# A twelve-stage network on one core: fill matmuls and high-part-first blocks behind norms, DeltaNet's roots, keys and masks by halves, retention's and cross-attention's outputs by two groups

## The reference

```python
# second block, each of four layers
h = h + rmsnorm_2(mixer(rmsnorm_2(h, g0)), g1)
h = h + rmsnorm_2(sq_relu_mlp(rmsnorm_2(h, g2), up, down), g3)
# DeltaNet (first block, layer 1), per head, chunks of 64
q, k = l2norm(q), l2norm(k)
decay = jnp.exp(jnp.where(tril, gcum[..., :, None] - gcum[..., None, :], -jnp.inf))
kkt = jnp.einsum('bhnid,bhnjd->bhnij', k * beta[..., None], k) * decay
# cross-attention and retention end with
x = x + o @ wo
y = merge_heads(rmsnorm_2(o)) * jax.nn.silu(g) @ w_out
```

## Time and profile before

| | us |
|---|---|
| median of 3 runs | 2855.59 (2853.14 to 2857.17) |
| the profiled execution | 2863.16 |
| its span | 2861.4 |
| PE busy in it | 2718.8 |
| DVE busy | 1812.8 |
| ACT busy | 1411.4 |

### The profile page before, as it was taken

How to read it: one execution, slowest core, us unless ns; L and a number is a source line. 1 busy time by engine, 2 the same in 40 slices (tenths; PEclk the granted TensorE clock), 3 DMA queues, 4 the chain that set the end, 5 groups by cost and what they waited for, 6 DMA issues and landing times. The chain is left out here.

```text
span 2861.4 us, 48984 instructions
## 1 busy us (share of the span) xinstructions
PE 2718.8 (95%) x21046; PEld 2625.2 (92%) x21046; DVE 1812.8 (63%) x2346; ACT 1411.4 (49%) x1924; POOL 0.2 (0%) x4
## 2 busy tenths in 40 slices
PE   7999999999997899999999999979999899999998
PEld 7999889999987889999998999879988899889998
DVE  5657656656656646666645855868455685655764
ACT  5445545454456354544445565454454544445543
POOL 0000000000000000000000000000000000000000
PEclk9999999999999999999999999989999999999999
DMA  6553535555543133555544454225542455444453
GB/s 213 177 187 131 174 123 192 187 184 189 182 143 111 67 125 128 192 187 170 170 147 148 162 192 164 73 96 189 191 148 92 149 199 187 155 153 140 155 198 126
DMA packets 129000, 450.09 MB, mean 157 GB/s; under 512 B 20112, under 2 KB 20368, under 8 KB 128528
## 3 DMA queue, kind: packets, MB, share of 16 engines
q1 hardware_dynamic: 128784, 446.96, 46.2%
HBM read 445.47 MB, written 1.44 MB: 156 GB/s over the span
## 5 line engine op out<-in xcount | busy, mean ns | idle before, releaser
L260 PE MATMUL B<-R,WH 128*128 128x256 f32 x10432 | 2103.6, 284 | 70.8 <-DVE R L977 39.6
L260 PEld LDWEIGHTS B<-R,WH 128*128 128x128 f32 x10432 | 1690.7, 191 | 87.8 <-DVE R L977 30.5
L911 DVE TENSOR_TENSOR WL<-SL,WH 128x1024 fp32r<-128x1024 f32 x836 | 1011.3, 1224 | 790.8 <-ACT WH L1935 789.4
L260 PE MATMUL B<-R,WL 128*128 128x256 f32 x4480 | 1264.9, 282 | 0.0
L1935 ACT ACTIVATE WH<-SL 128x1024 fp32r<-128x1024 f32 x836 | 865.7, 1052 | 583.8 <-PE B L260 468.5
L260 PEld LDWEIGHTS B<-R,WL 128*128 128x128 f32 x4480 | 855.5, 191 | 0.0
L260 PE MATMUL B<-RB,WH 128*128 128x256 f32 x1984 | 556.8, 281 | 0.0
L260 PE MATMUL B<-RB,WL 128*128 128x256 f32 x1728 | 482.5, 279 | 0.0
L260 PEld LDWEIGHTS B<-RB,WH 128*128 128x128 f32 x1984 | 373.8, 188 | 0.4
L260 PEld LDWEIGHTS B<-RB,WL 128*128 128x128 f32 x1728 | 324.2, 188 | 0.0
L260 PE MATMUL B<-WH,R 128*128 128x512 f32 x480 | 160.2, 403 | 1.1 <-DVE WL L911 1.1
(11 more groups left out here) (280 smaller groups left out, 1508.3 us busy)
## 6 DMA issues: line engine op xcount, KB each, us to landing
SL<-in_w SPq DMA_DIRECT2D x836, 512.0 KB, 3.6
CP<-in_cp SPq DMA_DIRECT2D x5, 768.0 KB, 4.9
X<-in_xT SPq DMA_DIRECT2D x2, 512.0 KB, 6.8
PG<-in_mem SPq DMA_DIRECT2D x1, 1024.0 KB, 10.9
out<-X SPq DMA_DIRECT2D x1, 1024.0 KB, 3.9
PK<-in_pk SPq DMA_DIRECT2D x1, 594.5 KB, 3.8
dn_y<-PG SPq DMA_DIRECT2D x1, 256.0 KB, 2.5
PG<-dn_y SPq DMA_DIRECT2D x16, 16.0 KB, 2.1
```

Source lines behind the costliest of these rows:

```text
L260: return p.matmul(o, left, right, start=first, stop=final, skip_group_check=True)
L911: v.tensor_tensor(WL[t % NSPL][:, :], SL[t % NRAW][:, :], WH[t % NSPL][:, :].bitcast(F32), ALU.subtract).then_inc(s_lo, 1)
```

## The change

1. `total` of the eight norms is followed by `keep(6)`: six fp32 matmuls of the identity with 256 columns of constants, into the next small bank. Nothing reads the result.
2. The block (0, 0) behind these norms waits for the input's high part alone, does four matmuls with it, and waits for the low part ahead of the last two. For the other blocks of group 0 the wait for the low part follows that for the high part.
3. r0.o and r3.o get `outer` 2. Head 2 is finished at (0, 1) (index 2), head 3 at (0, 5) (index 10), its sum is taken at (0, 4) (index 8).
4. DeltaNet: Ln, Exp and `normalize` of keys and queries by halves of 1024 columns; the keys' at index 43, the queries' at 75 and 79; DC's exponentials at 38, 39, 44 and 45; the products into L at 47 and 50, two each.
5. xk1a: `finish` at (0, 4), (0, 6), (1, 1), (1, 3), each followed one block later by `rest`; ACT's first copy of xk1a moves to (0, 7).
6. xk0: the second softmax by halves of four heads; its last parts at (1, 1) and (1, 3).
7. xo0 and xo1: group 1 is evacuated at (2, 1) (`landed`) and not at (1, 7), squares are added at k = 5 and not 3.

Its core:

```diff
-        outer = 2 if name in ("c.o", "g.o", "xo0", "xo1") else OUTER if name in ("f1.0.in", "r0.q", "c.in", "g.qk", "r3.q") or name.endswith(".up") else 0
+        outer = 2 if name in ("c.o", "g.o", "xo0", "xo1", "r0.o", "r3.o") else OUTER if name in ("f1.0.in", "r0.q", "c.in", "g.qk", "r3.q") or name.endswith(".up") else 0
...
+            def keep(n):
+
+                x = len(took)
+                b = 4 + x % 3
+                p.wait_ge(s_bank[b], x // 3)
+                for _ in range(n):
+                    mm(BK[b][:, 0:256], IDN, PK[:, 0:256])
...
-            def multiply(st, j, k, xh, xl):
+            def multiply(st, j, k, xh, xl, lower=None):
...
+                if lower is not None and j == 0 and k == 0:
+                    for half in range(2):
+                        o, ws = bk[:, cc(half)], slice(at + half * 128, at + half * 128 + 128)
+                        mm(o, hi[:, ws], xh, half == 0, False)
+                        mm(o, lo[:, ws], xh, False, False)
+                    lower(j, k)
+                    for half in range(2):
+                        t = mm(bk[:, cc(half)], hi[:, at + half * 128:at + half * 128 + 128], xl, False, False)
+                    t.then_inc(s_block, 1)
+                    return
+                if lower is not None:
+                    lower(j, k)
...
                 t.then_inc(s_sums, 1)
+                if n in POST and n < NN - 1:
+                    keep(6)
...
+                def lower(j, k):
+                    if j == 0:
+                        p.wait_ge(h_lo.sem, h_lo[n, k])
...
-                        p.wait_ge(h_lo.sem, h_lo[n, k])
+                        p.wait_ge(h_hi.sem, h_hi[n, k])
...
-                    if (j, k) == (0, 8):
+                    if (j, k) == (0, 4):
                         head_sums(3)
...
+        def landed(name, j, k):
+
+            last = k == ST[name].kc - 1
+            if ST[name].outer and j < 3:
+                return (0,) if last and j == 0 else (1,) if (j, k) == (2, 1) else (2,) if last and j == 2 else ()
+            return (j,) if last else ()
...
-                if j >= 2 and k == 3:
+                if j >= 2 and k == (5 if ST[name].outer else 3):
...
+                    S, w_, mx, sm = rows[min(x // 2, 1)]
+                    S3 = S.rearrange("p (n w) -> p n w", w=w_)
+                    if x in (0, 2, 3):
+                        at = slice(0, 8) if x == 0 else slice(4 * (x - 2), 4 * (x - 1))
+                        if x < 3:
+                            v.wait_ge(ab_exp.sem, ab_exp[x // 2])
+                        v.reduce_sum(sm[:, at], S3[:, at, :], AX).then_inc(V.sem, V.up())
+                        v.wait_ge(V.sem, V.n)
+                        v.reciprocal(sm[:, at], sm[:, at]).then_inc(V.sem, V.up())
+                    else:
+                        at = slice(0, 8) if x == 1 else slice(4 * (x - 4), 4 * (x - 3))
+                        v.wait_ge(V.sem, V.n)
+                        t = v.tensor_tensor(S3[:, at, :], S3[:, at, :], sm[:, at].unsqueeze(2).broadcast_to([128, at.stop - at.start, w_]),
+                                            ALU.mult)
+                        if x != 4:
+                            t.then_inc(ab_p.sem, ab_p.give(x // 5))
...
+                        part_of(k // 2)
+                    if (j, k) in ((1, 1), (1, 3)):
+                        part_of(4 + k // 2)
...
+                def normalize(key, x, base, scale):
+
+                    src = BIG[:, base + x * 1024:base + (x + 1) * 1024]
+                    v.wait_ge(dn_sd.sem, dn_sd[key, x])
+                    v.scalar_tensor_tensor(src, src, scale, PG[3][:, x * 1024:(x + 1) * 1024],
+                                           ALU.mult, ALU.mult).then_inc(dn_qk.sem, dn_qk.give((key, x)))
...
-                    if x == 46:
-                        normalize("k", BIG[:, 2048:4096], PG[3], 1.0)
-                    if 54 <= x < 58:
-                        q = x - 54
-                        if q == 0:
-                            v.wait_ge(dn_exp.sem, dn_exp["dc"])
-                        bk, free = had(("dkk", q))
-                        v.tensor_tensor(L[:, hc(q)], bk[:, :], DC[:, hc(q)], ALU.mult).then_inc(free, 1)
+                    if x == 43:
+                        normalize("k", 0, 2048, 1.0)
+                        normalize("k", 1, 2048, 1.0)
+                    if x == 47:
+                        v.wait_ge(dn_exp.sem, dn_exp["dc"])
+                    if x in (47, 50):
+                        for q in (0, 1) if x == 47 else (2, 3):
+                            bk, free = had(("dkk", q))
+                            v.tensor_tensor(L[:, hc(q)], bk[:, :], DC[:, hc(q)], ALU.mult).then_inc(free, 1)
...
+                    if x == 75:
+                        normalize("q", 0, 0, 128.0 ** -0.5)
...
-                    if x == 80:
-                        normalize("q", BIG[:, 0:2048], PG[3], 128.0 ** -0.5)
+                    if x == 79:
+                        normalize("q", 1, 0, 128.0 ** -0.5)
...
+                    if (j, k) in HEADS:
+                        finish(HEADS.index((j, k)))
+                    if (j, k - 1) in HEADS:
+                        rest(HEADS.index((j, k - 1)))
...
-                finish(2)
                 for j, k in to_post(r + ".o", n + 1):
-                    if (j, k) == (0, 7):
-                        finish(3)
+                    if j == 0 and k in (1, 5):
+                        finish(2 + k // 4)
...
-                    logs()
+                    if x:
+                        logs()
...
-                    a.activation(PG[3][:, :], PG[3][:, :], ACT.Ln, bias=pc("eps")).then_inc(A.sem, A.up())
+                    for y in range(2):
+                        s = PG[3][:, y * 1024:(y + 1) * 1024]
+                        a.activation(s, s, ACT.Ln, bias=pc("eps")).then_inc(A.sem, A.up())
...
-                    a.wait_ge(A.sem, A.n)
-                    a.activation(PG[3][:, :], PG[3][:, :], ACT.Exp, scale=-0.5).then_inc(dn_sd.sem, dn_sd.give("kq"[x]))
+                    for y in range(2):
+                        s = PG[3][:, y * 1024:(y + 1) * 1024]
+                        a.wait_ge(A.sem, A.n - 1 + y)
+                        a.activation(s, s, ACT.Exp, scale=-0.5).then_inc(dn_sd.sem, dn_sd.give(HALVES[2 * x + y]))
...
-                    if 44 <= x < 48:
-                        if x == 44:
-                            a.activation(BE, lnb, ACT.Exp).then_inc(dn_be.sem, dn_be.give("g"))
-                            a.wait_ge(dn_gc.sem, dn_gc["g"])
-                            a.activation(BEG, GC2, ACT.Exp).then_inc(dn_beg.sem, dn_beg.give("g"))
-                        exp_decay("dc", DC, GC2, x - 44)
+                    if x == 38:
+                        a.wait_ge(dn_gc.sem, dn_gc["g"])
+                        logs()
+                    if x in (38, 39, 44, 45):
+                        exp_decay("dc", DC, GC2, (38, 39, 44, 45).index(x))
+                    if x == 46:
+                        a.activation(BE, lnb, ACT.Exp).then_inc(dn_be.sem, dn_be.give("g"))
+                        a.activation(BEG, GC2, ACT.Exp).then_inc(dn_beg.sem, dn_beg.give("g"))
...
-                finish(2)
                 for j, k in to_post(r + ".o", n + 1):
-                    if (j, k) == (0, 7):
+                    if (j, k) == (0, 1):
+                        finish(2)
+                    if (j, k) == (0, 5):
                         sd(3)
                         finish(3)
```

More of the change, by code:

```diff
@@ L306, in multiply_tok, with gemm @@
                 t.then_inc(s_block, 2)
-            def gemm(name, hi, lo, hoff=0, loff=0):
+            def gemm(name, hi, lo, hoff=0, loff=0, lower=None):
                 st = ST[name]
@@ L333, in total @@
                 t.then_inc(s_sums, 1)
+                if n in POST and n < NN - 1:
+                    keep(6)
             def normed(name, n=None):
                 st = ST[name]
-                for j, k in gemm(name, R67, R67, 0, 2048):
+                def lower(j, k):
+                    if j == 0:
+                        p.wait_ge(h_lo.sem, h_lo[n, k])
+                for j, k in gemm(name, R67, R67, 0, 2048, None if n is None else lower):
                     if n is not None and (j, k) == ((3, 0) if st.outer else (1, 0)):
@@ L980, in out_group @@
             def out_group(name, j, k, n, scale, gain):
-                if j >= 2 and k == 3:
+                if j >= 2 and k == (5 if ST[name].outer else 3):
                     add_squares(n, j - 1)
[L983 to L986, removed]
+                for x in landed(name, j, k):
+                    bk, free = done(name, x)
+                    v.scalar_tensor_tensor(X[:, hc(x)], bk[:, :], scale, X[:, hc(x)], ALU.mult, ALU.add).then_inc(free, 1)
+                    evacuated(name, x)
                     if gain is not None:
-                        low(n, 2 * j, gain)
-                        low(n, 2 * j + 1, gain)
```

(44 more changed lines are left out.)

31 lines of the change are left out of this document (11 added, 20 removed).

## The result

| | before | changed |
|---|---|---|
| median of 5 runs, us | 2855.59 | 2841.07 |
| lowest to highest | 2853.14 to 2857.64 | 2836.39 to 2844.64 |
| profiled execution | 2863.16 (span 2861.4) | 2836.39 (span 2834.6) |
| mean granted clock in it | 0.980 | 0.992 |

The ratio is 0.9946 with a 95% interval of 0.9933 to 0.9959: 14.5 us faster, where 19.6 had been forecast, inside the recorded range. Run a second time beside other kernels, the change took 2841.98 us (0.9944, 0.9922 to 0.9966).

What follows compares the result with a forecast made beforehand. PE, busy for 95% of the span, was taken as the bound, so time could come only from its gaps and slow stretches. 4.3 + 10.4 + 6.5 + 1.4 - 1.0 - 2.0 = 19.6 us off 2855.59 gave 2836.0, range 2823 to 2850.

Steps and rivals of the forecast that it cites:

- Retention, +10.4: In r0.o and r3.o, two interleaved groups remove PE's waits for heads 2 and 3: 5.2 us gained in each.
- DeltaNet, +6.5: Halved, moved work on keys and queries shortens PE's waits: 6.5 us gained together, bounds 1 to 15.
- The second rival: DeltaNet gains nothing, as ACT is late and PE waits as long elsewhere: 2846, up to 2850; chance 0.20.
- the fourth: Rival: ACT is full in DeltaNet, PE waits for its squares at four places: 2867 us; chance 0.05.
- Fill and high part first, +4.3: Behind eight norms: r0.q gains 1.9, g.qk 0.8, r3.q 1.6 us, the other five places 0.
- five places at 0: The four ups and conformer's input: no gain, as DVE's chain sets a later wait.
- The first rival: Nothing is absorbed: the other five places behind norms pay too, up to 11.8 us more: 2824; chance 0.20.
- The third: Rival: the fill behind the norms does not hold the clock, its six matmuls take 5.1 us: 2853; chance 0.05.
- The wait at (5,4): In each up, PE still waits there for DVE's low part, 1.5 to 3 us instead of 0.8.
- xk0, +1.4: Softmax by halves brings a tile's low part some 2.1 us earlier, 0.7 waited again: 1.4 us gained (0.5 to 2.8).
- xk1a, -1.0: Heads spread out: the 3.10 us wait shrinks, the next tile's low part comes 1.1 later: 1.0 us lost.
- xo0 and xo1, -2.0: With the second group evacuated at (2,1), the last low part comes 1.0 us later, twice: 2.0 us lost.

Runs made afterwards that it cites:

- only_fill: The kernel before with the six fill matmuls behind the eight norms alone: 2857.45 us, ratio 0.9994 (0.9983 to 1.0006).
- undo_xo: The changed kernel with xo0 and xo1 evacuated and their squares added as before: 2842.25 us, ratio 0.9943 to the kernel before.
- only_two_groups: The kernel before with retention's output (r0.o, r3.o) by two groups alone: 2844.03 us, ratio 0.9961.
- undo_softmax_heads: The changed kernel with the old loops for xk0's softmax and xk1a's heads: 2842.44 us, ratio 0.9940 to the kernel before.

## Why the prediction was right

The measured median of 2841.07 us (2836.0 forecast) lies in the range, and the sign and the main mechanisms were right; some terms were off in size, and two places were misread.

- **Retention, +10.4.** 10.5 by the stages, 11.1 by the ratio. Right, for the reason given.
- **DeltaNet, +6.5.** 6.2 by dn.q and dn.z over fourteen profiles, 4.9 (1.7 to 8.3) by the ratio. The replay had three waits of about 3 us in the keys' part; the profile has 2.90, 1.74 and 1.84, ended by the normalised keys, ACT's gate and the last spread, and the second profile 2.90 and 3.01. The first wait became 1.23 us shorter, as the forecast's 1.25 had it; but the items listed for it (1.15 + 0.9 + 1.1 - 2.4) add up to 0.75. So the sum as written is wrong, and that its result came true is luck, or an item is missing from it. The queries' wait of 4.71 fell to 0.88, and 1.45 and 1.30 appeared behind it. The second rival (DeltaNet gains nothing) is excluded by the interval's lower end, 1.7. That ACT is full (the fourth) did not come: PE waits for its squares at two places, 871.51 and 890.21.
- **Fill and high part first, +4.3.** In m0.up the absorption is exact to 0.01 us (34.65 against 34.66). By the stages of the profile r0.q is 1.45 us shorter, r3.q 0.87, g.qk 0.05, and the stages ahead of them 0.44, 0.52 and 0.52 (the earlier start): 3.9. g.qk's 0.8 was mis-sized: little came but the start. Of the five places at 0, m0.up, m2.up and m3.up gave 0.3 to 0.5 us of the earlier start back within the stage. The other two were misread. m1.up had no wait at (5,4) before, and it lost 0.9 us more than it gained (in the second profile nothing). Conformer's input kept 0.9 us (0.5 in the second profile). They cancel. The two parts alone gave 0.6 and 0.7 us by the medians, 1.7 and 2.3 by the ratios, so the runs' times leave this term's size open. The first rival (all eight pay) is excluded: only_fill's interval ends at 4.9 us. The third (the fill does not hold the clock) is too: no half-clock stretch stands behind any of the eight fills.
- **The wait at (5,4)** was expected at 1.5 to 3 us; it is 1.1 to 1.2, with 0.3 at (2,6) and 0.6 at (3,0) ahead of it: what was saved is lost over three waits.
- **xk0, +1.4:** 1.5 in the mean of the profiles. In the changed profile the wait of 2.80 at one place is 0.67, 0.68 and 0.31 at three.
- **xk1a, -1.0:** -0.6 in xk1b, by the wait that was named (2.18 and then 1.25, where 3.10 was), and -1.0 more in xq1, which the forecast did not have: -1.6.
- **xo0 and xo1, -2.0:** over the six profiles with the new order against the eight with the old, f2.0.in takes 132.1 us, not 129.3, and f2.1.in 131.7, not 129.7, while xo1 is 0.6 shorter and xo0 too (26.8 against 27.4 in the three profiles that have the old order and the new softmax): -3.5. Without half-clock stretches it is 1.7 longer for each of the two; stretches fell in three of the six for each. The cause is also another one: the low-part wait that was to grow by 1.0 is 1.86 us with the new order and 1.88 with the old (undo_xo), and what came instead is a wait of 1.65 to 1.9 at (0,4). With xk1a it is what makes the change worse than it could be.

The terms add up to 10.5 + 6.2 + 3.9 + 1.5 - 1.6 - 3.5 = 17.0 us. The medians say 14.5 (11.7 to 19.1), and beside other kernels 15.6, or 16.0 by the ratio. So the forecast of 19.6 was 3.6 to 5.1 us too high. The two terms for xk1a, xo0 and xo1 account for 2.1 of that; the rest lies within the intervals and stays open. That the two profiles are 26.8 us apart is chance in good part: ab.v, which no edit touches, is 5.0 us of it, and dn.k 1.5.

## What to carry to other kernels

A pause that costs half clock is worth filling only if PE is what the next waits hang on; measure the time from the engine that sets the next wait, here DVE's 34.65 us from root to low part, before counting the clock. A need can be moved later instead of its supply earlier: two groups in turn over k doubled the time until a head was needed, at no cost that a stage shows, and that was nearly three quarters of the gain. Test the parts of a bundle alone and undone, since two of seven cost more than they gave; and look for the cost of a moved piece in the stages behind it too, as in xq1. Before a stage is compared, see what half-clock stretches and fast blocks fell in it, and take stages that no edit touches as the measure of chance.

## What the runs showed of the hardware that was not expected

**PE has two paces for the same stream at full clock.** The window from 2010 to 2080 us lies in m1.dn in both of these kernels, with PE busy throughout and a granted clock of 1.00 (length, busy us and count of PE, clock, DMA share, GB/s). Before:

```profile
2010.00:2080.00 70.00, 70.00 (x596) 1.00 0.56 187
```

only_two_groups:

```profile
2010.00:2080.00 70.00, 70.00 (x620) 1.00 0.63 208
```

One block takes 0.707 us in the first and 0.680 in the second, and nothing in between. In every profile the fast pace begins behind a block that took longer and lasts until a later one: in only_two_groups for 208 blocks of m1.up and m1.dn (208 x 0.027 = 5.6 us) and again for 208 of m3.up and m3.dn, in undo_softmax_heads for 208 of m0.up and m0.dn, in the first profile of the change nowhere over 19 blocks. The profile of before has some 60 fast blocks, the changed kernel some 30 and 190 in its two profiles, only_two_groups some 500. What decides it stays open. By an estimate from these two figures, the kernel's 2800 or so steady blocks would take 75 us less at the fast pace throughout, more than all that was tried here.

**Half-clock stretches come and go in stages that no edit touches.** ab.v had 10.2 us of them in the profile of before and took 25.9 us, none in the change's first (20.9), 10.2 again in its second (26.1). dn.k has 0, 3.4 or 6.8 us of them and takes 37.5, 39.0 or some 40.5. Runs of one kernel lie 10 us apart (2833.95 to 2844.32 in seven runs of the change). Effects of this size can make such a spread, though the runs without a profile do not show where their time went, and a single pair of profiles overstated the gain by 12 us.
